# A two-layer hybrid backbone: layer 1's outputs with two 64-token parts in one stationary tile, gates in runs of 32 tokens by expert pairs, another order in the first mixer's heads

## The chip, the cores and the metric

The kernel runs on one core of one Trainium2 chip. The metric is the device time of one execution in microseconds (us); lower is better.

## What is computed

Two layers over 256 latent tokens with 256 context tokens beside them, width 1024, float32. Layer 0 mixes tokens by a bidirectional gated linear recurrence (HGRN2, 8 heads of 128), layer 1 by sliding-window attention. Behind each mixer stands a PEER channel mixer: 8 heads pick 16 of 16384 experts for each token by product keys, and every chosen expert has one row of `u` and one of `v`. The core of the reference:

```python
def chunk(h):
    t = h.shape[0]
    q = (h @ wq).reshape(t, PEER_HEADS, 2, PEER_DQ // 2)
    s = jnp.einsum('thpd,hpnd->thpn', q, sub_keys).astype(F32)
    sv, si = lax.top_k(s, PEER_TOPK)
    ...
    idx = jnp.take_along_axis(cand_i, best, axis=-1)
    gate = jax.nn.softmax(best_s, axis=-1)
    act = jax.nn.gelu(jnp.einsum('td,thkd->thk', h, u[idx]).astype(F32))
    return jnp.einsum('thk,thkd->td', (gate * act).astype(v.dtype), v[idx])
```

Each sub-layer is `x <- LayerNorm(ALPHA * x + gate * f(x * (1 + scale) + shift))`, where the modulation comes from a product of the condition with `mod_w`.

## The kernel before

Everything is written out for each engine, with semaphores between them. Products with float32 accuracy are made of two parts: a tile is split into a high part (a copy in the reduced format fp32r, ScalarE) and a low part (the difference, VectorE or GpSimd), and three products high x high, high x low, low x high are summed.

**The heads of the first mixer** (`head` in each engine's program). For head h TensorE does the recurrence by 8 levels (line 896 and 890) and, between them, projects the next head: `proj_piece` (line 842, 12 products of 512 columns for each half of four column blocks) and `value_piece` (line 855, 24 products in four parts of six). Level l of VectorE multiplies queries and keys by their decays (lines 1683 to 1685), merges the level's products (1686), and ScalarE copies the keys for the next level (1279). Behind the levels follow key transposes (904), their copies (1295), state products (915), the states on VectorE (1703, 1705), the head's outputs (929), squares (1298) and their sums (935); `scale_head` and `finish` (1713) close a head. VectorE also makes eight sums of a modulation row with the condition (`mod_sum`, 1616) in each head, and `low_w` (1600), the low part of the next weights. SyncE loads a modulation row's block (565) as soon as the sum that frees its slot is made, and the weights of the head after next (573).

**PEER in full.** The chosen experts are spread over nearly all of the 16384, so for most tokens the kernel multiplies with every expert and weighs with a gate that is zero where an expert isn't chosen. 128 blocks of 128 experts pass by. The tokens for which this is done are 384 in layer 0 and 192 in layer 1 (`ND`); the others (128 and 64) gather their chosen rows by indirect loads (`rows`, 2263 and 2273), which VectorE multiplies and adds (2012, 2019, 2029, 2035) in the same loop. A step of the loop for block j: `u` and `v` are loaded (639, 641; SyncE's queue waits for `u_lo` before the next u and for `v_lo` before the next v, in this order); scores of block j+1 on TensorE (1032), GELU on ScalarE (1478), times the gates on VectorE (1995) into `prod`, its high part on ScalarE (1483) and low part on VectorE (1999); `u_hi`, `v_hi` on ScalarE (1391, 1481), `u_lo`, `v_lo` on VectorE (1975, 1997); then outputs of block j on TensorE, in layer 0 with the tokens as stationary operand (1092, moving 512 columns of v), in layer 1 with v as stationary operand (1086, moving 192 tokens), so that layer 1's result `yT` lies turned. The scores of the first `KA` = 24 blocks are made earlier, so that each layer's first 24 steps have outputs only.

**Gates.** A loop over 16 tokens at a time builds one-hot rows (VectorE 1970, 1971; weighed on ScalarE 1442 and GpSimd 2255), TensorE multiplies them (1075), ScalarE stores the products to `gb` (1455), and SyncE spills `gb` to the DRAM tensor `gd` (666). Within a block of experts `gb` and `gin` hold, for each of 32 tokens (`GCH`), four expert columns side by side. The last 32 tokens' gates are copied on chip (1489).

**The end.** Layer 1's `yT` is copied from its banks (ScalarE 1516, VectorE 2134), turned back (1124) and the 64 + 64 folded tokens joined (1120, 1127), then two blocks are normalised (1768 and following) and stored.

## Time and profile before

| | |
|---|---|
| runs shown | 2957.34, 2962.82, 2963.38 us; median 2962.82 us |
| profiled execution | 2962.92 us, its span 2961.1 us |
| TensorE busy | 2739.6 us (93%), mean granted clock 0.964 |
| VectorE busy | 2330.2 us (79%) |
| ScalarE busy | 1148.5 us (39%) |
| GpSimd busy | 847.1 us (29%) |
| HBM read, written | 635.31 MB, 45.92 MB; 230 GB/s over the span |
| chain that ended last | TensorE 17%, DMA 3%, VectorE 3% of the span |

Busy time is what the engine's instructions took; matmuls overlap, so that a full TensorE need not be at its peak. The chain of waits follows each step back to what released it, and covers the last part of the execution only. Engines are named PE (TensorE matmul), PEld (its weight load), DVE (VectorE), ACT (ScalarE), POOL (GpSimd) and SP (SyncE); SPq is its queue of transfers.

### The profile page before, as it was taken

What the parts mean: (1) busy time and instruction counts of PE and PEld (TensorE: products, weight loads), DVE (VectorE), ACT (ScalarE), POOL (GpSimd) and SP (SyncE); (2) the same over time, 40 slices, a digit from 0 to 9 for tenths busy, and PEclk for the clock granted to TensorE, in tenths of its full rate; (3) what the DMA queues carried; (4) which work ended last, traced back from release to release, by engine and by line L of the source; (5) the groups of instructions that cost most, each with busy time, mean ns of one, the idle gap of its engine ahead of it and who ended that gap; (6) DMA issues with size and microseconds to landing.
All of it is one profiled execution on the core that took longest, in us unless ns stands there. A gap on an engine that the chain in (4) does not pass through costs nothing. (4 is left out here: it accounts for less than half of the span.)

```text
span 2961.1 us, 46261 instructions
## 1 busy us (share of the span) xinstructions
PE 2739.6 (93%) x16594; PEld 2421.1 (82%) x16594; DVE 2330.2 (79%) x4148; ACT 1148.5 (39%) x1889; POOL 847.1 (29%) x565
## 2 busy tenths in 40 slices
PE   7999978899788999999999999798987899999997
PEld 3778864689777899999999999554887899999997
DVE  2788876799998778788888888743898877787887
ACT  2233320433583333333333333233446344444443
POOL 0000001435453344443333333000664212222221
PEclk9999988999999999999999999899898999999999
DMA  6223224415479998888888888311266978888885
GB/s 252 106 83 117 78 100 155 158 51 168 140 220 376 330 333 308 307 303 311 317 303 307 303 315 308 122 58 69 103 191 202 388 278 311 310 312 314 308 314 193
DMA packets 247822, 682.42 MB, mean 230 GB/s; under 512 B 20172, under 2 KB 106804, under 8 KB 244020
## 3 DMA queue, kind: packets, MB, share of 16 engines
q1 hardware_dynamic: 192436, 479.96, 46.2%
q0 software_dynamic: 55296, 201.35, 19.0%
q8 instruction: 45, 0.74, 0.1%
q14 instruction: 45, 0.37, 0.0%
HBM read 635.31 MB, written 45.92 MB: 230 GB/s over the span
## 5 line engine op out<-in xcount | busy, mean ns | idle before, releaser
L1032 PE MATMUL bank<-h_parts,u_hi 128*128 128x384 f32 (+1 forms) x3712 | 799.2, 307 | 21.8 <-DVE u_lo L1975 12.2
L1032 PEld LDWEIGHTS bank<-h_parts,u_hi 128*128 128x128 f32 x3712 | 627.0, 192 | 32.5 <-issue 12.6
L1032 PE MATMUL bank<-h_parts,u_lo 128*128 128x384 f32 (+1 forms) x1856 | 569.8, 307 | 0.0
L1092 PE MATMUL bank<-v_parts,p_hi 128*128 128x512 f32 x1536 | 477.2, 392 | 7.4 <-DVE p_lo L1999 7.4
L1086 PE MATMUL bank<-p_hi,v_parts 128*128 128x192 f32 x2048 | 371.2, 278 | 9.1 <-DVE p_lo L1999 8.4
L1032 PEld LDWEIGHTS bank<-h_parts,u_lo 128*128 128x128 f32 x1856 | 356.5, 192 | 0.0
L1997 DVE TENSOR_TENSOR v_parts<-arena,v_parts 128x1024 fp32r<-128x1024 f32 x256 | 313.2, 1223 | 36.3 <-ACT v_parts L1481 31.5
L1092 PEld LDWEIGHTS bank<-v_parts,p_hi 128*128 128x128 f32 x1536 | 288.0, 189 | 64.0 <-issue 7.6
L1086 PEld LDWEIGHTS bank<-p_hi,v_parts 128*128 128x128 f32 x2048 | 325.9, 195 | 12.9 <-DVE p_lo L1999 7.2
L1975 DVE TENSOR_TENSOR u_lo<-arena,u_hi 128x1024 fp32r<-128x1024 f32 x208 | 254.7, 1225 | 93.6 <-ACT u_hi L1391 89.7
L1391 ACT ACTIVATE u_hi<-arena 128x1024 fp32r<-128x1024 f32 x208 | 219.7, 1056 | 269.7 <-DMA arena<-in_u 269.3
L1478 ACT ACTIVATE arena<-bank 128x384 f32<-128x384 f32 (+1 forms) x208 | 85.2, 410 | 560.0 <-PE bank L1032 559.5
L1092 PE MATMUL bank<-v_parts,p_lo 128*128 128x512 f32 x768 | 301.8, 393 | 0.0
L1481 ACT ACTIVATE v_parts<-arena 128x1024 fp32r<-128x1024 f32 x256 | 269.6, 1053 | 78.4 <-PE bank L1092 47.1
L1995 DVE TENSOR_TENSOR arena<-arena 128x384 f32<-128x384 f32 (+1 forms) x256 | 175.3, 685 | 158.3 <-ACT arena L1478 144.2
L2263 POOL DMA_INDIRECT arena<-in_v,arena x128 | 197.1, 1540 | 320.9 <-DVE arena L2019 297.0
L1086 PE MATMUL bank<-p_lo,v_parts 128*128 128x192 f32 x1024 | 283.3, 277 | 0.0
L2263 POOL DMA_INDIRECT arena<-in_ug,arena x128 | 181.9, 1421 | 260.6 <-DVE arena L2012 237.2
L1086 PEld LDWEIGHTS bank<-p_lo,v_parts 128*128 128x128 f32 x1024 | 199.4, 195 | 0.0
L1075 PE MATMUL bank<-arena 128*128 128x128 f32 x1152 | 149.5, 285 | 33.7 <-DVE arena L1971 19.2
L1075 PEld LDWEIGHTS bank<-arena 128*128 128x128 f32 x1152 | 138.3, 197 | 45.2 <-ACT arena L1442 45.2
L842 PE MATMUL bank<-h_parts,u_hi 128*128 128x512 f32 x512 | 165.9, 405 | 5.0 <-DVE u_lo L1600 5.0
(308 smaller groups left out, 4630.4 us busy)
## 6 DMA issues: line engine op xcount, KB each, us to landing
arena<-in_u SPq DMA_DIRECT2D x256, 512.0 KB, 5.2
arena<-in_v SPq DMA_DIRECT2D x256, 512.0 KB, 4.4
arena<-in_wm SPq DMA_DIRECT2D x80, 512.0 KB, 4.2
arena<-in_wst SPq DMA_DIRECT2D x19, 2048.0 KB, 7.9
gate_scratch<-arena SPq DMA_DIRECT2D x18, 2048.0 KB, 8.7
arena<-gate_scratch SPq DMA_DIRECT2D x30, 768.0 KB, 6.6
arena<-in_whd SPq DMA_DIRECT2D x8, 2560.0 KB, 9.2
arena<-gate_scratch SPq DMA_DIRECT2D x30, 384.0 KB, 5.2
```

What stands on the lines that cost most here:

```text
L842: last = mm(out, w[:, k, :], x, start=(k == 0 and i == 0), stop=(k == KT - 1 and i == 2))
L1032: last = mm(banks[q][:, 0:ND[p]], w[:, q, col], h[:, k, DS[p]], start=(n3 == 0), stop=(n3 == 3 * KT - 1))
L1075: last = mm(out, tiles8(oh_i, q)[:, t, :], tiles8(oh_j, q)[:, t, :], start=True, stop=True)
L1086: last = mm(out, x[:, q, c * P:(c + 1) * P], y[:, q, 0:n_t], start=(first and i == 0 and c % 2 == 0), stop=(final and i == 2), skip_group_ ...
L1092: last = mm(banks[2 + 2 * b + half][:, :], x[:, q, b * P:(b + 1) * P], y[:, q, col], start=(first and i == 0), stop=(final and i == 2))
L1391: af_(u_hi[:, q, :], u_raw[:, q, :], ACT.Copy).then_inc(u_h[q], 1)
L1478: af_(act_s[:, q, 0:ND[p]], banks[q][:, 0:ND[p]], ACT.Gelu_apprx_tanh).then_inc(s_act[q], 1)
L1481: af_(v_hi[:, q, :], raw[:, q, :], ACT.Copy).then_inc(v_h[q], 1)
L1975: V.tensor_tensor(u_lo[:, q, :], u_raw[:, q, :], u_hi[:, q, :], ALU.subtract).then_inc(u_l[q], 1)
L1995: V.tensor_tensor(prod[:, q, 0:ND[p]], (act_s[:, q] if own else act_ring[r % 4])[:, 0:ND[p]], gates[:, 0:ND[p], r % 4], ALU.mult).then_inc ...
L1997: V.tensor_tensor(v_lo[:, q, :], raw[:, q, :], v_hi[:, q, :], ALU.subtract).then_inc(v_l[q], 1)
L2263: G.indirect_dma_start(rows[:, c, :], None, a["ug"].rearrange("l e d -> (l e) d") if x < PH * TOPK else a["v"].rearrange("l j i d -> (l j ...
```

## The change

Three things change.

1. Layer 1's outputs take the tokens as stationary operand. The high part of the 192 weights and the low part stand in one tile `p_parts`; its columns 192 to 319 (`p_two`) hold a second copy of the first 64 tokens' high part and, directly behind it, their low part. A product of `p_two` with `v_hi` and one with `v_lo` gives both parts' contributions on separate output rows of banks 4 and 5; the other 128 tokens have the three products on banks 2 and 3. At the end `foldw` adds the two row halves.
2. Gates lie as `(expert pair, token, 2)` in runs of 32 tokens.
3. In the heads of the first mixer some products and sums stand elsewhere.

```diff
         h_hi, h_lo = h_parts[:, 0, :, :], h_parts[:, 1, :, :]
-        p_hi = sb("p_hi", [P, 2, ND_MAX], F32R)
-        p_lo = sb("p_lo", [P, 2, ND_MAX], F32R)
+        p_parts = sb("p_parts", [P, 2, 2 * ND_MAX], F32R)
...
-        gb = ar(B_HF, 8192, s=2, j=NK // 4, t=GCH, f=4)
+        gb = ar(B_HF, 8192, s=2, n=NK // 2, t=GCH, f=2)
...
+        PL = [ND_MAX, 256]
...
+        def p_hi(p):
+            return p_parts[:, :, 0:ND[p]]
+        def p_lo(p):
+            return p_parts[:, :, PL[p]:PL[p] + ND[p]]
+        p_two = p_parts[:, :, ND[1]:ND[1] + P]
...
                     if l == 0:
                         pe.wait_ge(init, h + 1)
-                    if more:
+                    if more and l != 1:
                         proj_piece(h + 1, l // 2, l % 2)
...
                     last.then_inc(lvl, 1)
+                    if more and l == 1:
+                        proj_piece(h + 1, 0, 1)
+                if more:
+                    value_piece(h + 1, 0, 2)
                 pe.wait_ge(upd, 7 * h + 7)
...
                     last.then_inc(kt_pe, 1)
                 if more:
-                    value_piece(h + 1, 0)
+                    value_piece(h + 1, 2, 3)
...
                     last.then_inc(ds, 1)
-                    if more:
-                        value_piece(h + 1, 1 + d)
+                if more:
+                    value_piece(h + 1, 3, 6)
...
                 if more:
-                    value_piece(h + 1, 3)
+                    value_piece(h + 1, 6, KT)
...
                     if p:
-                        n_t = ND[p]
-                        for c in range(KT):
-                            out = banks[2 + c // 2][:, (c % 2) * n_t:(c % 2 + 1) * n_t]
-                            for i, (x, y) in enumerate(((v_hi, p_hi), (v_hi, p_lo), (v_lo, p_hi))):
-                                last = mm(out, x[:, q, c * P:(c + 1) * P], y[:, q, 0:n_t], start=(first and i == 0 and c % 2 == 0),
-                                          stop=(final and i == 2), skip_group_check=True)
-                    for b in range(0 if p else nd):
+                        for half in range(2):
+                            for i, y in enumerate((v_hi, v_lo)):
+                                mm(banks[4 + half][:, :], p_two[:, q, :], y[:, q, 512 * half:512 * half + 512],
+                                   start=(first and i == 0), stop=(final and i == 1))
+                    for b in range(nd - p):
                         for half in range(2):
                             col = slice(half * 512, half * 512 + 512)
-                            for i, (x, y) in enumerate(((p_hi, v_hi), (p_hi, v_lo), (p_lo, v_hi))):
-                                last = mm(banks[2 + 2 * b + half][:, :], x[:, q, b * P:(b + 1) * P], y[:, q, col],
+                            at = p * HALF + b * P
+                            for i, (x, y) in enumerate(((p_hi(p), v_hi), (p_hi(p), v_lo), (p_lo(p), v_hi))):
+                                last = mm(banks[2 + 2 * b + half][:, :], x[:, q, at:at + P], y[:, q, col],
                                           start=(first and i == 0), stop=(final and i == 2))
...
-                    pe.wait_ge(modT_a, 5)
-                    pe.wait_ge(at_oc, 11)
-                    for c in range(KT):
-                        last = nc.tensor.transpose(banks[c // 4][:, (c % 4) * P:(c % 4 + 1) * P], yT[:, c, P:2 * P], ident)
-                    last.then_inc(y_pe, 1)
...
+                    for half in range(2):
+                        last = mm(banks[6 + half][:, :], foldw[:, 0:P], y_two[:, 512 * half:512 * half + 512], start=False, stop=True)
...
-                        dst = gb[:, c, :, t0:t0 + 4, :].rearrange("p j t f -> p t j f")
+                        dst = gb[:, c, :, t0:t0 + 4, :].rearrange("p n t f -> p t n f")
...
+                    if p:
+                        af_(p_two[:, q, 0:HALF], prod[:, q, 0:HALF], ACT.Copy)
...
             def levels(h, slot, more, more2):
+                mod_sum(h, 0, 0)
                 if more:
                     low_w(h + 1, 1 - slot, 1)
-                mod_sum(h, 0, 0)
...
-                    if l % 2:
+                    if l in (1, 3, 5):
                         mod_sum(h, 2 + l // 4, (l // 2) % 2)
...
                 finish(h, slot)
+                mod_sum(h, BLOCKS_M - 1, 1)
...
-                    V.memset(yT[:, :, 0:HALF], 0.0).then_inc(at_oc, 1)
...
-                    norms(3, LN_BASE[p], LAST, lambda i, half: banks[6 * i + half][:, :], lambda b: 1, [8 + Y_BLOCK[1][1] + 1, 8 + Y_BLOCK[1][1] + 2])([0, 1])
+                    norms(3, LN_BASE[p], LAST, lambda i, half: banks[2 + 4 * i + half][:, :], lambda b: 1, [0, 8 + Y_BLOCK[1][1] + 1])([0, 1])
```

The multiply by the gates is rewritten to `gates[:, 0:ND[p] // GCH, (r % 4) // 2, :, r % 2]`: before, a step's gate of one token lay four numbers from the next token's, now two.

TensorE, in a head of the first mixer, from behind the key transposes (line 904, then 915) to the sums of squares (935, then 946). The value products of the next head are at line 855, then 863; the state products at 915, then 926; the outputs at 929, then 940. Before:

```order
L855 MATMUL bank<-h_parts,v_parts 128x512 x6
L911 REGISTER_ALU
L912 REGISTER_ALU
L915 MATMUL bank<-arena 128x128 x3
L855 MATMUL bank<-h_parts,v_parts 128x512 x6
L915 MATMUL bank<-arena 128x128 x3
L855 MATMUL bank<-h_parts,v_parts 128x512 x6
L929 MATMUL bank<-arena 128x128 x10
L855 MATMUL bank<-h_parts,v_parts 128x512 x6
L935 MATMUL bank<-const,arena 128x1 x4
```

and now, from the value products in front of the transposes:

```order
L863 MATMUL bank<-h_parts,v_parts 128x512 x6
L915 MATMUL bank<-const,arena 128x128 x3
L912 REGISTER_ALU
L915 MATMUL bank<-const,arena 128x128 x3
L863 MATMUL bank<-h_parts,v_parts 128x512 x3
L922 REGISTER_ALU
L923 REGISTER_ALU
L926 MATMUL bank<-arena 128x128 x6
L863 MATMUL bank<-h_parts,v_parts 128x512 x9
L940 MATMUL bank<-arena 128x128 x10
L863 MATMUL bank<-h_parts,v_parts 128x512 x6
L946 MATMUL bank<-const,arena 128x1 x4
```

Six value products now stand ahead of the transposes, three between them and the state products, and nine between the state products and the outputs.

TensorE at the end of layer 1's loop: the last output products of layer 1 (line 1086, then 1095 and 1102) and the joining of the folded tokens. Before:

```order
L1086 MATMUL bank<-p_lo,v_parts 128x192
L1086 MATMUL bank<-p_hi,v_parts 128x192 x2
L1086 MATMUL bank<-p_lo,v_parts 128x192
L1086 MATMUL bank<-p_hi,v_parts 128x192
L1120 MATMUL bank<-arena 128x512 x2
L1124 MATMUL bank<-const,arena 128x128 x8
L1127 MATMUL bank<-const,arena 128x128 x8
```

and now, for the last two blocks of experts:

```order
L1095 MATMUL bank<-v_parts,p_parts 128x512 x4
L1102 MATMUL bank<-v_parts,p_parts 128x512 x6
L1095 MATMUL bank<-v_parts,p_parts 128x512 x4
L1102 MATMUL bank<-v_parts,p_parts 128x512 x6
L1130 MATMUL bank<-arena 128x512 x2
L1134 MATMUL bank<-arena 128x512 x2
```

A block has ten products of 512 columns instead of 24 of 192, and the sixteen products that turned the result back are replaced by two.

VectorE from a head's end (`finish` 1713, then 1721) into the next head's start; a conditioning sum is line 1616, then 1624. Before:

```order
L1713 SCALAR_TENSOR_TENSOR arena<-bank,small,arena 128x512
L1722 REGISTER_ALU
L1724 ISA
L1724 TENSOR_TENSOR modcol<-small,modcol 128x8
L81 REGISTER_ALU
L1599 REGISTER_ALU
L1600 TENSOR_TENSOR u_lo<-arena,u_hi 128x1024
L1612 ISA
L1613 REGISTER_ALU
L1616 ISA v_parts,small<-arena 128x1024
L1616 ISA small 128x1
```

and now, from the same place:

```order
L1721 SCALAR_TENSOR_TENSOR arena<-bank,small,arena 128x512
L1624 ISA v_parts,small<-arena 128x1024
L1624 ISA small 128x1
L1731 REGISTER_ALU
L1733 ISA
L1733 TENSOR_TENSOR modcol<-small,modcol 128x8
L81 REGISTER_ALU
L1620 ISA
L1621 REGISTER_ALU
L1624 ISA v_parts,small<-arena 128x1024
L1624 ISA small 128x1
```

One sum stands behind the head's end now, and the next head's first sum stands ahead of `low_w`.

## Rows read from the trace of the kernel before

**Rows 1.** Windows, layer 0's and layer 1's expert loop: busy us of each engine, clock, DMA, GB/s

```profile
1030.00:1400.00 370.00, 370.00 (x1875) 337.17 (x1874) 296.10 (x395) 131.45 (x180) 160.82 (x109) 1.00 0.89 314
2850.00:2900.00 50.00, 50.00 (x450) 50.00 (x450) 40.52 (x48) 24.82 (x39) 12.72 (x10) 1.00 0.90 310
```

**Rows 2.** Chain that ended last, layer 1's loop: start, length (us), work

```profile
2393.98 2.68 PE bank L1032 x24
...
2849.84 2.68 PE bank L1086 x24
...
2932.92 2.69 PE bank L1032 x24
```

**Rows 3.** Timeline, VectorE and TensorE, one head: start, length, engine, line, operation [idle before]

```profile
318.22 0.75 DVE L1713 SCALAR_TENSOR_TENSOR arena<-bank,small,arena 128x512 f32 x1
...
332.24 1.23 PE L896 MATMUL bank<-arena 128*128 128x128 f32 x8 [1.12 <-ACT arena L1279]
...
353.50 0.88 PE L904 MATMUL bank<-const,arena 128*128 128x128 f32 x6 [1.55 <-DVE arena L1685]
...
358.25 1.64 PE L855 MATMUL bank<-h_parts,v_parts 128*128 128x512 f32 x6
359.72 2.42 PE L929 MATMUL bank<-arena 128*128 128x128 f32 x20
...
363.35 0.75 DVE L1713 SCALAR_TENSOR_TENSOR arena<-bank,small,arena 128x512 f32 x1
```

**Rows 4.** Timeline, TensorE in layer 0's loop: first output and first score products

```profile
1507.21 0.63 PE L1092 MATMUL bank<-v_parts,p_hi 128*128 128x512 f32 x2
1511.33 0.51 PE L1032 MATMUL bank<-h_parts,u_hi 128*128 128x384 f32 x2
```

**Rows 5.** Timeline, one step of layer 1's loop, by engine

```profile
2853.42 0.34 SPq L639 DMA_DIRECT2D arena<-in_u  x1
2858.06 1.06 ACT L1391 ACTIVATE u_hi<-arena 128x1024 fp32r<-128x1024 f32 x1 [1.29 <-DMA arena<-in_u]
2859.71 1.23 DVE L1975 TENSOR_TENSOR u_lo<-arena,u_hi 128x1024 fp32r<-128x1024 f32 x1
2863.08 0.38 PE L1032 MATMUL bank<-h_parts,u_hi 128*128 128x192 f32 x2
```

**Rows 6.** Transfers of 2400 to 2900 us, and the chain's longest landing there

```profile
DMA packets 43362, 154.95 MB, mean 310 GB/s; under 512 B 4814, under 2 KB 4814, under 8 KB 43355
arena<-in_u SPq DMA_DIRECT2D x93, 512.0 KB, 5.3
...
2427.64 7.59 DMA arena<-in_u
```

**Rows 7.** Windows and transfers at the start of layer 1's experts

```profile
2308.00:2330.00 22.00, 21.66 (x178) 20.46 (x179) 22.00 (x39) 10.90 (x15) 6.78 (x7) 1.00 1.03 401
...
arena<-in_v SPq DMA_DIRECT2D x23, 512.0 KB, 9.1
```

**Rows 8.** Groups by line and shape: busy us, mean ns | idle before

```profile
L1997 DVE TENSOR_TENSOR v_parts<-arena,v_parts 128x1024 fp32r<-128x1024 f32 x256 | 313.2, 1223 | 36.3 <-ACT v_parts L1481 31.5
...
L1455 ACT ACTIVATE arena<-bank 128x512 f32<-128x512 f32 x144 | 76.8, 579 | 4.0 <-PE bank L1075 3.9
...
L1995 DVE TENSOR_TENSOR arena<-arena 128x192 f32<-128x192 f32 x128 | 64.9, 507 | 24.7 <-ACT arena L1478 17.6 <-DMA arena<-gate_scratch 6.1
...
L1999 DVE TENSOR_TENSOR p_lo<-arena,p_hi 128x192 fp32r<-128x192 f32 x128 | 45.1, 352 | 0.0
```

**Rows 9.** Timeline, VectorE at a head's first level

```profile
328.70 0.69 DVE L1683 TENSOR_TENSOR arena<-arena 128x512 f32<-128x512 f32 x1 [0.44 <-PE bank L896]
329.31 1.15 DVE L1684 TENSOR_TENSOR arena<-arena 128x512 f32<-128x512 f32 x1
```

**Rows 10.** Timeline, VectorE at the kernel's end

```profile
2941.47 1.02 DVE L2134 COPY arena<-bank 128x384 f32<-128x384 f32 x2 [0.43 <-PE bank L1086]
2944.15 1.29 DVE L1768 TENSOR_TENSOR arena<-bank,arena 128x512 f32<-128x512 f32 x2 [1.66 <-PE bank L1124]
```

More of the change, by code:

```diff
@@ L65 @@
 C_KEEP, C_ALL = 384, 1024 + 256
-C_SHIFT, C_FOLD, C_END = C_ALL, C_ALL + 192, C_ALL + 192 + 128
+C_SHIFT, C_FOLD, C_END = C_ALL, C_ALL + 192, C_ALL + 192 + 192
 HALF = P // 2
@@ L334, in build @@
         oh_j = ar(6144, 2048, s=2, d=D)
-        gin = ar(4096, 3072, s=2, t=ND_MAX, f=4)
-        gin_first = [ar(at, 4 * ND_MAX, t=ND_MAX, f=4) for at in (B_Q, B_M)]
+        gin = ar(4096, 3072, s=2, c=ND_MAX // GCH, h=2, t=GCH, f=2)
+        gin_first = [ar(at, 4 * ND_MAX, c=ND_MAX // GCH, h=2, t=GCH, f=2) for at in (B_Q, B_M)]
         act_s = ar(8192, 768, s=2, t=ND_MAX)
@@ L348, in build @@
         s20 = ar(9984, 20)
-        yT = ar(A_HD, 2 * D, c=KT, t=2 * P)
+        y_two = ar(A_HD, D)
         shift = ar(B_T + 1152, 192)
-        foldw = ar(B_T + 1536, P)
-        assert B_T + 1536 + P <= AW and A_HD + 2 * D <= A_LN
+        foldw = ar(B_T + 1536, P + HALF)
+        assert B_T + 1536 + P + HALF <= AW and A_HD + D <= A_LN
         p16 = ar(10004, 16)
@@ L665, in spill @@
                     rows = gate_rows(c)[:, j0:j1, :]
-                    sp.dma_start(rows, gb[:, c % 2, j0:j1, :, :].rearrange("p j t f -> p j (t f)")).then_inc(g_out[c % 2], 16)
+                    sp.dma_start(rows, gb[:, c % 2, 2 * j0:2 * j1].rearrange("p (j h) t f -> p j (h t f)", h=2)).then_inc(g_out[c % 2], 16)
                 for c in range(C):
@@ L844, in proj_piece, with value_piece @@
                     last.then_inc(proj, 1)
-            def value_piece(g, part):
+            def value_piece(g, k0, k1):
                 w_hi, w_lo = weight_parts(2)
-                if part == 0:
+                if k0 == 0:
                     pe.wait_ge(hw_l, 5 * g + 5)
@@ L852, in value_piece @@
                         pe.wait_ge(vsb, 2 * g)
-                for k in range(2 * part, 2 * part + 2):
+                for k in range(k0, k1):
                     for i, (w, x) in enumerate(((w_hi, h_hi[:, k, :]), (w_hi, h_lo[:, k, :]), (w_lo, h_hi[:, k, :]))):
                         last = mm(banks[7][:, :], w[:, k, :], x, start=(k == 0 and i == 0), stop=(k == KT - 1 and i == 2))
-                if part == 3:
+                if k1 == KT:
                     last.then_inc(vproj, 1)
@@ L868, in _ @@
                     proj_piece(0, c, half)
-            for part in range(4):
-                value_piece(0, part)
+            value_piece(0, 0, KT)
             def head(h, slot, more):
@@ L1119, in peer @@
                     for half in range(2):
-                        mm(banks[6 + half][:, :], foldw, y_tok[:, 512 * half:512 * half + 512], start=True, stop=False, skip_group_check=True)
-                    pe.wait_ge(modT_a, 5)
-                    pe.wait_ge(at_oc, 11)
-                    for c in range(KT):
-                        last = nc.tensor.transpose(banks[c // 4][:, (c % 4) * P:(c % 4 + 1) * P], yT[:, c, P:2 * P], ident)
-                    last.then_inc(y_pe, 1)
-                    for c in range(KT):
-                        last = mm(banks[6 + c // 4][:, (c % 4) * P:(c % 4 + 1) * P], yT[:, c, 0:P], ident, start=False, stop=True, skip_group_check=True)
+                        mm(banks[6 + half][:, :], foldw[:, HALF:HALF + P], y_tok[:, 512 * half:512 * half + 512], start=True, stop=False)
+                    pe.wait_ge(modT_a, 4)
+                    pe.wait_ge(at_oc, 9)
+                    for half in range(2):
+                        last = mm(banks[6 + half][:, :], foldw[:, 0:P], y_two[:, 512 * half:512 * half + 512], start=False, stop=True)
                     last.then_inc(y_pe, 1)
@@ L1514, in peer @@
                     act.wait_ge(y_ac[1], 1 + PAIRS * 2)
-                    for x in range(2):
-                        af_(yT[:, 2 * x:2 * x + 2, HALF:2 * P], banks[2 + x][:, 0:2 * ND[p]].rearrange("p (c t) -> p c t", c=2), ACT.Copy).then_inc(modT_a, 1)
+                    af_(y_two[:, 0:512], banks[4][:, :], ACT.Copy).then_inc(modT_a, 1)
             peer(0)
@@ L1763, in front @@
                     st = stat[:, (i % 4) * 20:(i % 4) * 20 + 20]
-                    if y_need:
+                    if y_need and y_need[i]:
                         dve.wait_ge(y_pe, y_need[i])
@@ L1994, in step @@
                         dve.wait_ge(g_first, 2 * p + slot + 1)
-                    V.tensor_tensor(prod[:, q, 0:ND[p]], (act_s[:, q] if own else act_ring[r % 4])[:, 0:ND[p]], gates[:, 0:ND[p], r % 4], ALU.mult).then_inc(p_do[q], 1)
+                    weights, gelus = (x[:, 0:ND[p]].rearrange("p (c t) -> p c t", t=GCH) for x in (prod[:, q], act_s[:, q] if own else act_ring[r % 4]))
+                    V.tensor_tensor(weights, gelus, gates[:, 0:ND[p] // GCH, (r % 4) // 2, :, r % 2], ALU.mult).then_inc(p_do[q], 1)
                     dve.wait_ge(v_h[q], N + 1)
@@ L2132, in peer @@
                     dve.wait_ge(y_ac[1], 1 + PAIRS * 2)
-                    for x in range(2):
-                        V.tensor_copy(yT[:, 4 + 2 * x:6 + 2 * x, HALF:2 * P], banks[4 + x][:, 0:2 * ND[p]].rearrange("p (c t) -> p c t", c=2)).then_inc(at_oc, 1)
+                    V.tensor_copy(y_two[:, 512:1024], banks[5][:, :]).then_inc(at_oc, 1)
                 if p == 0:
```

14 lines of the change are left out of this document (7 added, 7 removed).

## The prediction, made before the changed kernel ran

> **What bounds the kernel now.** I read the views in this order: busy time by stretch, to see which engine is full in which stage; the chain that ended last, for the step of layer 1's expert loop; the timeline of one step there and of one head; the groups by shape for the prices; and the transfers of two stretches.
>
> Layer 0's expert loop is full on TensorE: 370.00 of 370 us, VectorE at 296 [rows 1]. Its matmuls do not change, so a faster multiply on VectorE buys nothing there. Layer 1's loop is full on TensorE too, 50.00 of 50 us, while VectorE is busy 40.5 and the transfers run at 310 GB/s [rows 1]. Its step is 24 score products and 24 output products of 192 columns, 2.68 us each set; from 2393.98 to 2932.92 there are 100 steps, so 5.389 us a step, against 2 x 2.68 = 5.36 if nothing ever waited [rows 2]. TensorE thus loses 3 us in 100 steps.
>
> The first mixer's heads repeat every 363.35 - 318.22 = 45.13 us, and in each TensorE stands still twice: 1.12 us before the second level's products, 1.55 us before the key transposes [rows 3]. The rest of a head is matmuls.
>
> **Part 1, layer 1's outputs.** Removed in each of 128 steps: 24 matmuls of 192 columns, 2.68 us [rows 2]. That is 112 ns each although they have few columns to stream. Added: ten of 512 columns, four with the 64 tokens' high and low halves side by side as one stationary tile, six for the other 128 tokens. Layer 0 has this shape: 18 of them take 1511.33 - 1507.21 = 4.12 us, or 229 ns each [rows 4]. Ten cost 2.29 us, so the step would be 2.68 + 2.29 = 4.97 us. The Trainium skill (TensorE: Matmul & The Clock Gate, "Wait — 56ns, not 53.3ns?") puts a matmul at N / 2.4 GHz + 2.5 ns, 216 ns for 512 columns; by it ten would cost 2.16 us, the step 4.84, and the loop 13 us less than by the row. No row here shows 216, so I keep the row's 229.
>
> Who is late next? VectorE's work of a step is 40.5 / 50 x 5.36 = 4.3 us [rows 1], so it isn't VectorE. It is the u block. In the step shown it is issued at 2853.42, ScalarE starts on it at 2858.06, VectorE ends u_lo at 2859.71 + 1.2 = 2860.9, and TensorE takes it at 2863.08, 2.2 us later [rows 5]. The issue follows v_lo of step j (SyncE waits for it at line 641 before the next u) and the use is the scores of step j + 3, so the allowance is three steps less a fixed part. Three steps of 0.39 us less take 1.17 us from it. Issue to use is 9.66 us here; less 1.06 for u_hi and 1.2 for u_lo, a landing of up to 7.4 us is borne now, and 6.2 to 6.5 then. The median landing is 5.3 us and single ones take 7.59 [rows 6]. Pairing each of the loop's issues with ScalarE's start on that block, as in [rows 5], I count 12 of 95 above 6.5 us, together 7.4 us over: 0.08 us a step. Landings also lengthen with traffic: a step moves 310 GB/s x 5.389 us = 1.67 MB [rows 6], so 326 GB/s at 5.13 us. At 401 GB/s, in layer 1's first steps, a block lands after 9.1 us [rows 7]; between (310, 5.3) and (401, 9.1) that is about 0.6 us more at 326, which brings the loss to some 0.16 us a step. I take 5.13 us: 5.389 - 5.13 = 0.26 us, x 100 = **26 us**. The ends: 42 us if no block is ever late (4.97), 0 if the landing holds the old pace.
>
> The other 24 steps, at layer 1's start, have outputs only. There VectorE is busy 22.00 of 22 us and the transfers run at 401 GB/s with a share over 1 [rows 7]. TensorE isn't the bound and the bytes stay: 0 us. Layer 1's ScalarE gets one more copy a step (64 columns); it costs less than the 579 ns of a 512-column copy and runs while VectorE makes v_lo (1223 ns), so 0 us [rows 8]. If that cover went, up to 0.58 us x 100 would be at stake.
>
> **Part 2, gates by pairs.** The multiply reads a gate each 16 bytes now and takes 507 ns for 192 columns, against 352 for the same-sized subtraction with dense reads [rows 8]. It will read each 8 bytes. A VectorE product of 512 columns with such reads takes 0.69 us [rows 9], no more than dense ones, so I expect about 0.35 us: 0.15 us off VectorE in layer 1, 0.3 in layer 0. VectorE sets neither loop, so 0 us. The gate stage's ScalarE stores write runs of two numbers instead of four; 579 ns now [rows 8]. I take no change, since runs of two appear in the levels without loss; the other end is below, among the rivals.
>
> **Part 3, heads.** (a) Six value products (358.25 to 359.72, 1.47 us [rows 3]) move in front of the key transposes, into the wait of 1.55: 1.47 us gained. They must not be missed later: behind the state products nine now stand in one run (2.2 us) where VectorE computes the states, so the outputs still find TensorE the last. (b) At level 1 the products of the next head go behind the level's own. VectorE's 0.44 us wait for these [rows 9] goes, the next key copy comes as much earlier, and TensorE's 1.12 us shrink to about 0.7: 0.44 us. (c) On VectorE one conditioning sum goes from before the states to behind the head's end, another fills a wait at the head's start. VectorE holds no end there: 0 us, but the sum frees the 1.2 us that (a) needs. Its weight row's load is issued that much later, on SyncE's queue just ahead of the next head's 2.5 MB; it is used some 6 us later, so hidden. Together 1.9 us x 7 heads = **13.3 us**. Ends: 0 and 2.67 x 7 = 18.7 us.
>
> **Part 4, the end.** Block 3's norm reads its banks directly instead of waiting 1.66 us for the turned-back block, and one bank copy of about 0.5 us is gone from VectorE (two took 1.02) [rows 10]: about **2.2 us**; ends 0 and 2.7. One clearing write goes from the loop, once; I leave it out.
>
> Sum: 26 + 13.3 + 2.2 = 41.5 us off the profiled execution's 2962.92 us (2961.1 its span), which equals the median of 2962.82 within 0.1: **2921 us**.
>
> **The rivals.**
> (B) The u blocks are never late. For: after each late one the spare recovers within two steps. Against: the 7.59. Loop 42 us, total 57.5: 2905 us.
> (C) The transfers hold the loop. For: in the step shown ScalarE stands 1.29 us until u has landed [rows 5], and the traffic rises as the step shortens. Against: 401 GB/s is reached elsewhere [rows 7], at which 1.67 MB need 4.2 us. If the landings lengthen so much that the step stays near 5.33, the loop gives 6 us and the total is 21.5: 2941 us. The Trainium skill (DMA: Bandwidth & Descriptors, "Where 436 GB/s comes from") puts the limit of loads from HBM near 358 GB/s a core, which would put (C) closer: 1.67 MB would need 4.7 us. The trace disagrees, with 401 GB/s over 22 us.
> (D) The heads' waits only move, as VectorE becomes their last: 2934 us.
> (E) Slower: the gate stores with runs of two. The steepest row for short runs is VectorE's first level, 1.15 us against 0.69, where every element lies apart [rows 9]. At that ratio a store takes 0.97 us, +0.39 x 144 = 56 us with nothing hidden, and the total is 2977 us. It decides from 42 / 144 = 0.29 us a store. Against: later levels, with runs of two and more, do not show it. The Trainium skill (SBUF — State Buffer, "Door 1: The DMA port swizzle (why `[64,N]` ≈ `[32,N]`)") speaks of 16-byte lines that need two hits for full bandwidth; by it runs of two numbers stay at full speed, and the 16-byte reads of the multiply, one hit each, are the slow ones, with which the 507 ns agree.
>
> **How the numbers follow.** Forecast 0.58, (B) 0.17, (C) 0.15, (D) 0.05, (E) 0.05. What a measurement of this kernel can tell from no change is about 0.2%, 6 us. All but (E) are faster by more; a part of (C) might fall within, were the heads to fail with it: faster 0.92, same 0.03, slower 0.05. The range reaches from a little below (B), 2903, to a little above (C), 2945.
>
> **What would show it.** Right: layer 1's outputs at 2.3 us for ten matmuls; the loop's step 5.0 to 5.25 us, with TensorE's waits there on VectorE's u_lo, and ScalarE waiting for in_u before them; the multiply near 0.35 us; a head of 43.2 us; layer 0's outputs unchanged at 4.12 us; stores near 579 ns; the end 2 us shorter. Wrong: a step of 5.33 with long waits for in_u (C), stores above 0.8 us (E), heads at 45 (D), or matmuls of 512 columns at another price than 229 ns behind those of 192.

## The result, and the profile after

| | before | changed |
|---|---|---|
| median of the runs | 2963.1 us (4 runs, 2957.3 to 2965.3) | 2944.1 us (4 runs, 2941.0 to 2947.5) |
| profiled execution, and its span | 2962.92, 2961.1 | 2943.2, 2941.4 |
| ratio of changed to before | | 0.9936, 95% interval 0.9920 to 0.9952 |

The change takes 19 us off, 14 to 24 by the interval. 41.5 were forecast. The profile's page of the changed kernel, its busy times and the chain that ended last:

```profile
PE 2698.3 (92%) x14782; PEld 2307.4 (78%) x14782; DVE 2279.4 (77%) x4146; ACT 1159.3 (39%) x2016; POOL 849.8 (29%) x565
...
DMA 9%; PE 6%; DVE 5%; issue 3%; ACT 2%; SPq 1%; DVEq 0%; ACTq 0%; POOLq 0%
DMA arena<-in_u 7%; PE bank L1043 3%; DVE v_parts L2007 2%; PE bank L1102 1%; ACT u_hi L1398 1%; PE bank L1095 1%; DVE u_lo L1984 1%; ACT v_parts L1488 1%; DVE arena L2039 1%; PE bank L1086 1%; DVE arena L1980 0%; DMA arena<-gate_scratch 0%; DVE arena L2005 0%; SPq L649 0%; DMA arena<-in_v 0%
```

Before, TensorE was 17% of the span in that chain. Now the load of u leads it with 7%. The windows say the same, in the columns of [rows 1]: layer 0's loop is as full as it was, layer 1's no longer.

```profile
1200.00:1570.00 370.00, 370.00 (x1871) 336.71 (x1870) 291.74 (x371) 127.72 (x180) 148.58 (x98) 1.00 0.88 308
2850.00:2900.00 50.00, 48.85 (x326) 43.26 (x326) 39.07 (x50) 27.59 (x50) 11.90 (x10) 1.00 0.89 320
```

Taken step by step from the starts of the score products, an undisturbed step of layer 1's loop is 4.96 us, as forecast. But the last 100 steps, up to the one that starts at 2915.47, take 524.9 us, 5.249 each, against 5.389 before: 14 us saved, not 26. 24 of these steps are over 5.26 us, and 15 of these stand at a multiple of four steps from each other: 28.9 us are lost in the hundred, where before it was 2.9.

The 19.7 us between the two profiled spans lie as follows: 0.6 are there when layer 1's outputs begin (2286.9 before, 2286.3 now), 2.7 come up to the last 100 steps, 14.0 in these, 2.4 behind the last scores. So in this pair of profiles next to nothing of the heads' gain had come through to layer 1's outputs, though the heads themselves did what was forecast. VectorE and TensorE, one head, the timeline's columns as in [rows 3]:

```profile
309.03 0.74 DVE L1721 SCALAR_TENSOR_TENSOR arena<-bank,small,arena 128x512 f32 x1
...
322.66 1.23 PE L903 MATMUL bank<-arena 128*128 128x128 f32 x8 [0.64 <-ACT arena L1286]
...
343.93 0.87 PE L915 MATMUL bank<-const,arena 128*128 128x128 f32 x6 [0.16 <-DVE arena L1693]
...
352.22 0.74 DVE L1721 SCALAR_TENSOR_TENSOR arena<-bank,small,arena 128x512 f32 x1
```

A head takes 352.22 - 309.03 = 43.19 us. The waits of 1.12 and 1.55 us [rows 3] have become 0.64 and 0.16, and the last head ends at 440.7 instead of 454.6: 13.9 us. The groups by shape for the multiply, the gate stores and the added copy [rows 8], and VectorE at the end [rows 10]:

```profile
L2005 DVE TENSOR_TENSOR arena<-arena 128x192 f32<-128x192 f32 x128 | 45.2, 353 | 10.5 <-DMA arena<-gate_scratch 7.7 <-ACT arena L1485 2.8
...
L1462 ACT ACTIVATE arena<-bank 128x512 f32<-128x512 f32 x144 | 78.6, 594 | 4.0 <-PE bank L1086 3.8
...
L1491 ACT ACTIVATE p_parts<-arena 128x64 fp32r<-128x64 f32 x128 | 32.8, 256 | 41.6 <-DVE arena L2005 40.2
```

```profile
2923.83 0.69 DVE L2142 COPY arena<-bank 128x512 f32<-128x512 f32 x1
2924.44 1.28 DVE L1777 TENSOR_TENSOR arena<-bank,arena 128x512 f32<-128x512 f32 x2
```

The multiply went from 507 to 353 ns, the stores from 579 to 594, and at the end one bank copy and the wait of 1.66 us are gone.

Two questions: what holds the u blocks back, and where do 14 us of the heads go?

### The profile page after: what moved, and what is told of

It is laid out like the page before. It is cut to its first block and busy times, and to the rows that moved or that the text cites. A ratio compares the mean times of both kernels' runs of the same rounds, so it can differ in the third digit from the quotient of the medians.

```text
span 2941.4 us, 42761 instructions
## 1 busy us (share of the span) xinstructions
PE 2698.3 (92%) x14782; PEld 2307.4 (78%) x14782; DVE 2279.4 (77%) x4146; ACT 1159.3 (39%) x2016; POOL 849.8 (29%) x565
## 5 line engine op out<-in xcount | busy, mean ns | idle before, releaser
L1102 PE MATMUL bank<-v_parts,p_parts 128*128 128x512 f32 x3072 | 747.0, 393 | 8.9 <-DVE p_parts L2009 8.9
L1102 PEld LDWEIGHTS bank<-v_parts,p_parts 128*128 128x128 f32 x3072 | 580.0, 189 | 129.3 <-issue 7.3
L2271 POOL DMA_INDIRECT arena<-in_v,arena x128 | 198.9, 1554 | 319.0 <-DVE arena L2029 295.2
L2271 POOL DMA_INDIRECT arena<-in_ug,arena x128 | 176.1, 1376 | 270.7 <-DVE arena L2022 246.6
L2005 DVE TENSOR_TENSOR arena<-arena 128x384 f32<-128x384 f32 (+1 forms) x256 | 117.0, 457 | 150.9 <-ACT arena L1485 132.5
L1086 PE MATMUL bank<-arena 128*128 128x128 f32 x1152 | 150.0, 286 | 33.2 <-DVE arena L1980 19.7
L2029 DVE SCALAR_TENSOR_TENSOR arena<-arena 128x1024 f32<-128x1024 f32 x128 | 164.0, 1281 | 6.8
L1095 PE MATMUL bank<-v_parts,p_parts 128*128 128x512 f32 x512 | 147.0, 410 | 16.5 <-DVE p_parts L2009 16.5
L2022 DVE CUSTOM_DVE_ANT_0 arena<-arena 128x1024 f32<-128x1024 f32 x128 | 151.4, 1219 | 2.8 <-DMA arena<-in_ug,arena 2.8
L2281 POOL DMA_INDIRECT arena<-in_v,arena x64 | 74.2, 1160 | 264.6 <-DVE arena L2045 240.2
L2281 POOL DMA_INDIRECT arena<-in_ug,arena x64 | 81.7, 1276 | 211.3 <-DVE arena L2039 207.4
```

What stands on the lines that cost most here:

```text
L1086: last = mm(out, tiles8(oh_i, q)[:, t, :], tiles8(oh_j, q)[:, t, :], start=True, stop=True)
L1095: mm(banks[4 + half][:, :], p_two[:, q, :], y[:, q, 512 * half:512 * half + 512], start=(first and i == 0), stop=(final and i == 1))
L1102: last = mm(banks[2 + 2 * b + half][:, :], x[:, q, at:at + P], y[:, q, col], start=(first and i == 0), stop=(final and i == 2))
L2029: V.scalar_tensor_tensor(y_tok, rows[:, x % RING_G, :], p16[:, x:x + 1], y_tok, ALU.mult, ALU.add).then_inc(row_use[x % RING_G], 1)
L2271: G.indirect_dma_start(rows[:, c, :], None, a["ug"].rearrange("l e d -> (l e) d") if x < PH * TOPK else a["v"].rearrange("l j i d -> (l j ...
L2281: G.indirect_dma_start(rows[:, c, :], None, a["ug"].rearrange("l e d -> (l e) d") if x < HALF else a["v"].rearrange("l j i d -> (l j i) d" ...
```

## The experiments: which part gives what

All ratios are against the kernel before, run beside them on the same chip.

**e1, the heads alone.** The kernel before, with only this part of the change:

```diff
 def head(h, slot, more):
-    if more:
+    if more and l != 1:
         proj_piece(h + 1, l // 2, l % 2)
...
+    if more and l == 1:
+        proj_piece(h + 1, 0, 1)
+ if more:
+    value_piece(h + 1, 0, 2)
  pe.wait_ge(upd, 7 * h + 7)
...
-    if l % 2:
+    if l in (1, 3, 5):
         mod_sum(h, 2 + l // 4, (l // 2) % 2)
...
  finish(h, slot)
+ mod_sum(h, BLOCKS_M - 1, 1)
```

> The kernel before with the heads' part of the change alone (order of the next head's products and of the conditioning sums); outputs and gates as before. Both theories expect a head of 43.2 us and wout's start about 14 us earlier, as in the changed kernel. Theory S (swallowed): the later stages (key scores and top-k with GpSimd, the outputs-only steps at the transfers' pace) wait for something that the heads do not move, so little of it reaches the end: -1 to -4 us, and the last scores of layer 0's loop start no more than 3 us earlier than before. Theory F (forecast): the 13.3 us arrive at the end, -11 to -15 us, and what the changed kernel lost behind the heads was lost by its own gate stage and outputs.

Measured: 2949.8 us median of 5, ratio 0.9948 (0.9935 to 0.9961), so 12 to 19 us faster. Theory S falls: in its profile the last output product of layer 0's loop starts 7.0 us earlier than in the kernel before (1857.1 against 1864.1), where theory S allowed 3. The heads' gain does reach the end, at least its greater part.

**e2, all but the heads.** The changed kernel with the diff of e1 taken back.

> The changed kernel with the heads as before. Theory S: almost the changed kernel's time, -15 to -19 us against the kernel before. Theory F: the heads carry about 13 us of the change's 19, so only about -6 us are left.

Measured: 2954.7 us median of 10 (2944.7 to 2963.6), ratio 0.9971 (0.9957 to 0.9985), so 4 to 13 us faster. Outputs, gates and end together give some 9 us, where 28.2 were forecast. In its profile layer 1's step is 5.303 us. Its runs spread over 19 us, which would fit a loop that hangs on single landings; no run shows that this is the reason.

**e3, the gates alone.** The kernel before with the layout of `gin` and `gb` changed, and the multiply:

```diff
-gb = ar(B_HF, 8192, s=2, j=NK // 4, t=GCH, f=4)
+gb = ar(B_HF, 8192, s=2, n=NK // 2, t=GCH, f=2)
...
-... gates[:, 0:ND[p], r % 4], ALU.mult)
+... gates[:, 0:ND[p] // GCH, (r % 4) // 2, :, r % 2], ALU.mult)
```

> The kernel before with the gates in runs by expert pairs alone. The multiply falls from 507 to 353 ns (192 columns) and from 863 to 561 (384). Forecast: no effect on the time, within 3 us, since VectorE sets neither loop. Rival: the stores in runs of two (594 against 579 ns) lie on the gate stages' path, 144 x 15 ns = 2 us slower, to +5 us; and if the multiply lies on the way from the transfers to the products, 3 to 8 us faster.

Measured: ratio 1.0003 (0.9994 to 1.0011). The multiply takes 355 and 560 ns, a store 592, and the time stands still. VectorE's saved time is worth nothing in either loop.

**e9, the changed kernel again**, to see how far it scatters.

> The changed kernel itself, word for word, beside the others: how far its own time scatters. Expected 2941 to 2948 us, within the interval seen. With the same kernel without the heads' part at 2954.7 it says what the heads are worth at the end: 10 us or more bears out the forecast's term of 13.3, under 5 us would not.

Measured: 2940.1 us median of 6 (2932.5 to 2954.0), ratio 0.9916 (0.9897 to 0.9934), 1 us below the expected 2941 to 2948. Against e2 that is 14.6 us less, and it agrees with the sum of e1 and e2. The profiled execution was its slowest, 2954.0. Its profile once more shows nothing of the heads' gain where layer 1's outputs begin (2291.6 us). But these two profiles are the exception: with the heads' change the outputs begin at 2275.1 to 2281.4 us in the eight others, and without it at 2285.5 to 2287.7 in all four. So one pair of profiles can mislead by several us about what a part is worth. Here the many runs decide, and they give the heads 12 to 19 us and the rest 4 to 13.

## The experiments: what makes the u blocks late

The trace of the changed kernel shows a stall. SyncE's queue, and then ScalarE, VectorE and TensorE with the block whose load is issued last here:

```profile
2653.78 0.33 SPq L649 DMA_DIRECT2D arena<-in_v  x1
2654.31 0.33 SPq L643 DMA_DIRECT2D arena<-gate_scratch  x1
2654.84 0.33 SPq L647 DMA_DIRECT2D arena<-in_u  x1
```

```profile
2663.38 1.06 ACT L1398 ACTIVATE u_hi<-arena 128x1024 fp32r<-128x1024 f32 x1 [4.10 <-DMA arena<-in_u]
```

```profile
2664.47 1.23 DVE L1984 TENSOR_TENSOR u_lo<-arena,u_hi 128x1024 fp32r<-128x1024 f32 x1 [3.14 <-ACT u_hi L1398]
```

```profile
2665.75 0.47 PE L1043 MATMUL bank<-h_parts,u_hi 128*128 128x192 f32 x2 [1.98 <-DVE u_lo L1984]
```

Two things stand in front of this u: the wait for v_lo with v's 512 KB behind it, and 384 KB of gates, which are loaded every fourth step. ScalarE can start on it only 8.5 us after its issue. I paired all issues of the loop with ScalarE's starts. The 23 blocks right behind a gates load take 6.64 us in the mean, the 67 others 5.59. In the kernel before it was 6.43 (23) and 5.27 (69). I had read this spread as scatter; it has a period. Where TensorE's lateness falls says the same: the steps that use the 23 blocks behind gates carry 17.8 of some 28 us lost.

**e4, u issued ahead of the wait for v_lo.** Bytes and buffers stay; only SyncE's order in layer 1's loop changes (one load ahead of the loop, none of u in its last step):

```diff
+def experts_ahead(j, q, N):
+    nq, nN = 1 - q, N + q
+    sp.wait_ge(u_l[nq], 1 + nN)
+    sp.dma_start(u_raw[:, nq, :], a["u"][p, j + 1]).then_inc(u_in[nq], 16)
+    sp.wait_ge(v_l[q], 1 + N)
+    sp.dma_start(v_raw[:, q, :], a["v"][p, j]).then_inc(v_in[q], 16)
```

> The changed kernel, with each u block of layer 1's loop issued on SyncE before the wait for v_lo that it stood behind, some 2 us earlier; same bytes, same buffers. Theory L (landing: the block has too little time from issue to use): the step falls from 5.25 to 4.97-5.08 us, 17 to 28 us over 100 steps, and the time is 2917 to 2927 us. Theory B (bytes: 16 DMA engines cannot move 1.67 MB a step faster beside the gathers): the step stays at 5.2 to 5.3, the time within 3 us of 2944, and ScalarE waits for in_u or in_v as long as now.

Measured: 2909.1 us median of 5, ratio 0.9807 (0.9795 to 0.9820), 35 us below the changed kernel's first median and 31 below that of e9. That is more than theory L forecast (2917 to 2927). The step is 4.967 us over the last 100, one of them late. SyncE's queue and ScalarE in its profile:

```profile
2645.15 0.33 SPq L654 DMA_DIRECT2D arena<-in_u  x1
2647.35 0.33 SPq L656 DMA_DIRECT2D arena<-in_v  x1
```

```profile
2652.19 1.06 ACT L1413 ACTIVATE u_hi<-arena 128x1024 fp32r<-128x1024 f32 x1 [0.77 <-DMA arena<-in_u]
```

u now goes out 2.2 us ahead of v instead of 0.5 us or more behind it. ScalarE still waits for in_u, and the way from issue to its start isn't shorter, 6.8 us in the mean against 5.9: the wait has just moved to where it is covered. Theory L holds and B falls, since more bytes a second pass: 337 GB/s against 316. The windows from 2500 to 2850 us, of the kernel before, the changed one, e5 (below) and e4:

```profile
2500.00:2850.00 350.00, 349.47 (x3119) 348.61 (x3119) 283.55 (x357) 171.81 (x263) 82.39 (x65) 1.00 0.87 311
```

```profile
2500.00:2850.00 350.00, 336.05 (x2252) 301.06 (x2251) 274.45 (x362) 183.09 (x331) 75.22 (x66) 1.00 0.89 316
```

```profile
2500.00:2850.00 350.00, 344.00 (x2314) 308.07 (x2313) 281.68 (x370) 188.84 (x342) 76.70 (x68) 1.00 0.90 325
```

```profile
2500.00:2850.00 350.00, 349.59 (x2392) 320.74 (x2391) 296.53 (x379) 192.11 (x353) 110.19 (x71) 1.00 0.93 337
```

**e5, the gates behind the u block.** The changed kernel, with the wait and load of the gates called inside `experts`, between u and v:

```diff
 sp.dma_start(u_raw[:, q, :], a["u"][p, j]).then_inc(u_in[q], 16)
+if gate:
+    gate()
 sp.wait_ge(v_l[q], 1 + N)
```

> The changed kernel, but in layer 1's loop every fourth step's load of gates (384 KB) is issued behind that step's u block instead of ahead of it; the u block still stands behind the wait for v_lo. In the changed kernel the 23 u blocks issued just behind a gates load take 6.64 us from issue to ScalarE's start in the mean, the 67 others 5.59. Theory G (the queue: it is the 384 KB in front that make a u block late): these 23 fall to about 5.6, most stalls of every fourth step go, the step is 5.05 to 5.12 us, the time 2924 to 2934 us. Theory W (the wait for v_lo alone: a u block's time is too short wherever the gates stand): the stalls only move to other steps, within 4 us of 2944.

Measured: 2924.9 us median of 5, ratio 0.9882 (0.9867 to 0.9897), 19 us below the changed kernel's first median and 15 below that of e9. The step is 5.147 us, and 18.7 us are lost in 100 instead of 28.9. The time lies where theory G put it, the step above its 5.05 to 5.12. The same 23 blocks take 6.0 us instead of 6.6, not the 5.6 of the forecast, and the others 5.7 instead of 5.6. The loss in the steps that use these 23 falls from 17.8 to 5.4 us, and in the others it rises from 10.0 to 12.2. So each theory has a share: most of what the gates caused goes, and a part moves to other steps. The gates in front account for about a third of the loss by the profiles, for about half of e4's gain by the medians (0.3 to 0.4 of it by the ratios). The rest is the place behind the wait for v_lo.

**e6, the kernel before with the edit of e4.**

> The kernel before with u issued ahead of the wait for v_lo in layer 1's loop (the edit of e4 without the change). The step stands at TensorE's 5.36 us already, with 3 us lost in 100 steps. If e4's 35 us are slack that only the shorter step needs, this gives -1 to -4 us against the kernel before. If e4's gain were something else (less traffic at a time, fewer collisions), it would show here too, with more than -8 us.

Measured: ratio 0.9991 (0.9982 to 1.0000), median 2960.6 of 12. The step is 5.364 us, TensorE's pace. The same edit that is worth 31 to 35 us behind the change is worth 3 without it (0 to 5 by the interval): the old step hid the late blocks.

**e8, both.** e4, and the gates between u and v.

> e4 with the gates load issued behind the u block as well. Its step is at TensorE's 4.96 us in all but one place, so nothing is left to take: within 3 us of e4's 2909. If v blocks had become late behind the earlier u, it would be slower by some us.

Measured: 2906.3 us median of 5, ratio 0.9817 (0.9803 to 0.9832). The same as e4 within what can be told. e4 and e8 beat both kernels by far: 54 to 58 us below the kernel before, by the medians.

**e7, two output products fewer**, to see how far the transfers could follow. It leaves out one of the three terms for the last 128 tokens.

```diff
-for i, (x, y) in enumerate(((p_hi(p), v_hi), (p_hi(p), v_lo), (p_lo(p), v_hi))):
+products = ((p_hi(p), v_hi), (p_hi(p), v_lo), (p_lo(p), v_hi))[:3 - p]
+for i, (x, y) in enumerate(products):
```

> e4 with two of layer 1's ten output products of a step left out: the product of the low weights with the high v rows for the last 128 tokens (they are missing from the output). TensorE's step is then 2.68 + 8 x 0.229 = 4.51 us, VectorE's work in it stays near 4.2. Theory B (bytes hold just below e4's pace): 1.67 MB in 4.51 us would be 370 GB/s; if the transfers stop at some 340 to 360 GB/s, the step is 4.65 to 4.9 and TensorE waits for u or v. Theory R (room left): the step is 4.51 to 4.6, -36 to -45 us in the loop against e4, and the transfers run at 360 to 370 GB/s. The Trainium skill (DMA: Bandwidth & Descriptors, 'Where 436 GB/s comes from') has the loads of a core at about 358 GB/s, by which theory B would hold, at 4.66 us.

Measured: 2883.5 us median of 4, ratio 0.9741 (0.9726 to 0.9755). The step is 4.654 us over the last 100, 4.51 undisturbed.

```profile
2500.00:2800.00 300.00, 295.40 (x2058) 266.86 (x2057) 266.33 (x348) 179.49 (x325) 89.06 (x65) 1.00 0.96 359
```

Between the two theories, and nearer to B: most steps run at 4.51, but some in each stretch are late, and the mean stays at 359 GB/s, with a share of 0.96. So 6% below e4's step something beside TensorE begins to hold. The Trainium skill (DMA: Bandwidth & Descriptors, "Where 436 GB/s comes from") has about 358 GB/s for the loads of a core. The mean here comes out at that number, but it is no ceiling for this core, since 401 passed over 22 us [rows 7]. That the bytes are what holds is not shown. VectorE, busy 266 of 300 us, isn't far from full here either, and the time from a u block's issue to its use has fallen to 9.6 us in the mean, from 11.6 in e4. This run doesn't part the three.

## The experiments: the heads

**e10, level 1 as before.** The changed kernel with `if more and l == 1` taken back, so that the next head's products stand ahead of the level's own again.

> The changed kernel, but at level 1 the next head's products stand ahead of the level's own again, as before. Forecast: the wait ahead of the second level's products returns to about 1.1 us (0.64 in the changed kernel), and a head takes 43.6 us instead of 43.19. Rival: the wait is not set by that order, and the head stays at 43.2.

Measured in a single execution: the wait is 1.11 us again.

```profile
323.92 1.23 PE L903 MATMUL bank<-arena 128*128 128x128 f32 x8 [1.11 <-ACT arena L1284]
```

Of the seven distances between its head ends five are 43.61 to 43.96 us, where in the changed kernel five are 43.19 to 43.25. So the term of 0.44 us holds, in kind and in size. From the first head end to the last it is 307.5 us against 305.5, but that sum decides nothing: over the eight other profiles with the same heads it runs from 304.5 to 307.9, since now and then a head is about 1 us longer. (Its 2940.2 us of a single execution say nothing about 3 us.)

**e11, the last conditioning sum as before.**

```diff
-    if l in (1, 3, 5):
+    if l % 2:
         mod_sum(h, 2 + l // 4, (l // 2) % 2)
...
- mod_sum(h, BLOCKS_M - 1, 1)
```

> The changed kernel, but with VectorE's last conditioning sum of a head ahead of the states again instead of behind the head's end. Forecast (the sum frees the 1.2 us which the six value products in front of the key transposes need behind them): the state products' readers are late, and a head takes 44.0 to 44.4 us. Rival (VectorE had the time anyway): 43.2 to 43.4.

Measured in a single execution (2939.3 us): five of the seven distances are 43.50 to 43.54 us, 0.3 longer than in the changed kernel and between the forecast and the rival. VectorE at the first state behind TensorE's state products, in the changed kernel and then in e11:

```profile
303.02 0.29 DVE L1711 COPY arena<-bank 128x128 f32<-128x128 f32 x1 [0.59 <-PE bank L926]
```

```profile
303.25 0.28 DVE L1711 COPY arena<-bank 128x128 f32<-128x128 f32 x1
```

In the changed kernel VectorE still waits 0.59 us for the products there; in e11 it comes last itself. So the sum's new place is worth about 0.3 us a head, less than the 0.8 to 1.2 expected, and the value products' gain hangs on it only in this part.

**Where profiles lose what the heads gain.** At the first early scores the profiles with the heads' change are still 9 to 15 us ahead. In the stretch from there to the gates' one-hot rows VectorE selects experts while GpSimd computes low parts. It takes 115.8 us in the kernel before and 120.8 in e1 and in the changed kernel (119.5 in e2, so that it isn't the heads' change alone that can lengthen it). The windows of before and of e1 over it:

```profile
655.60:771.40 115.80, 105.39 (x585) 104.01 (x585) 110.90 (x382) 36.90 (x52) 60.29 (x23) 0.94 0.47 157
```

```profile
641.50:762.30 120.80, 107.83 (x585) 106.45 (x585) 115.91 (x382) 36.83 (x52) 60.14 (x23) 0.92 0.46 150
```

VectorE executes the same 382 instructions and is busy 5.01 us longer, which is the whole difference. Single ones stretch. GpSimd and VectorE of e1, and then the same two operations in the kernel before:

```profile
710.56 2.40 POOL L2252 TENSOR_TENSOR u_lo<-arena,u_hi 128x1024 fp32r<-128x1024 f32 x1 [3.15 <-ACT u_hi L1403]
```

```profile
711.01 2.51 DVE L1919 CAST arena<-arena 128x1024 f32<-128x1024 uint32 x1
```

```profile
719.67 2.40 POOL L2248 TENSOR_TENSOR u_lo<-arena,u_hi 128x1024 fp32r<-128x1024 f32 x1 [0.29 <-ACT u_hi L1400]
```

```profile
723.26 0.68 DVE L1915 CAST arena<-arena 128x1024 f32<-128x1024 uint32 x1
```

The copy that takes 0.68 us alone takes 2.51 when a GpSimd operation began 0.45 us ahead of it, and ends 0.56 us after that one's end (712.96). In seven of the nine profiles with the heads' change before e12 the copy is hit so (2.51 to 2.56 us), in e8's and e11's it takes 0.68, as in all four without. The stretch goes with it: from the first early scores to the one-hot rows it is 120.7 or 120.8 us in all seven, and 115.6 and 115.8 in e11 and e8, though these have the heads' change too. The window of e8:

```profile
645.40:761.30 115.90, 105.48 (x585) 104.10 (x585) 111.00 (x382) 36.88 (x52) 60.31 (x23) 0.94 0.48 157
```

Of the 5 us the copy itself has 1.9; in the same profiles other operations of VectorE stretch too, one of 4096 columns from 5.16 to 6.48 us. (The expectation below counts ten and three, one too many.) The Trainium skill (SBUF — State Buffer, "SBUF: two separate sides") says that VectorE and GpSimd share a pair of ports, and that the one which starts first, on VectorE's side an operation in a two-port mode or with two inputs in SBUF, holds it for the whole instruction while the other blocks. The trace agrees.

**e12, the copy moved.** e8, with this copy ahead of the sum, the reciprocal and the product that it followed:

```diff
+link(V.tensor_copy(si..., siu...))
 dve.wait_ge(ex_a, p + 1)
 link(V.tensor_reduce(gsf, bsf, AX.X, ALU.add))
```

> e8 with one of VectorE's copies (uint32 to float, 1024 columns, in layer 0's selection of experts) moved 1.2 to 2 us earlier, ahead of the sum, reciprocal and product it followed. In the profiles of seven of the ten kernels with the heads' change this copy takes 2.5 us and ends 0.55 us after the GpSimd operation that began up to 0.5 us before it; in the three others and in all without that change it takes 0.68, and the stretch from the first early scores to the gates is 5 us shorter. Theory K (VectorE stands still while GpSimd's operation holds what they share; which copies are hit is a matter of phase): the copy takes 0.68 us there and the stretch is 115.5 to 117 us; the time is 0 to 5 us below e8's 2906. Rival (the copy is a symptom, the stretch is longer for another reason, such as the granted clock): the copy is short and the stretch is still 120 to 121 us.

Measured: 2909.5 us median of 5, ratio 0.9820 (0.9805 to 0.9835), e8's time. The stretch takes 117.6 us, but the copy isn't short. GpSimd and VectorE:

```profile
704.73 2.40 POOL L2283 TENSOR_TENSOR u_lo<-arena,u_hi 128x1024 fp32r<-128x1024 f32 x1 [0.30 <-ACT u_hi L1431]
708.88 2.89 POOL L2283 TENSOR_TENSOR v_parts<-arena,v_parts 128x1024 fp32r<-128x1024 f32 x1 [1.76 <-ACT v_parts L1434]
```

```profile
705.50 2.17 DVE L1939 CAST arena<-arena 128x1024 f32<-128x1024 uint32 x1
...
709.55 2.31 DVE L1948 COPY arena<-arena 128x128 f32<-128x128 f32 x1
```

Both signs of theory K failed, the copy of 0.68 us and the stretch of at most 117, and the rival's too. The copy met another GpSimd operation, and ended 0.54 us after it (707.13). A copy of 128 columns was hit as well, and GpSimd's operation beside it took 2.89 us instead of 2.40. That fits the rule, read afterwards, and it shows that moving one operation doesn't free the stretch. Which ones are hit seems a matter of phase; a remedy would have to take work off one of the two engines there, and wasn't tried. The changed kernel's profile loses in two more places. Between the last head and the first early scores it loses 3.7 us, nearly all in the stretch that starts with the key scores, where TensorE is busy 103.6 of 109.2 us before and 105.7 of 112.7 now. In the four profiles with a mean granted clock of 0.95 or 0.96 there (the changed kernel, e8, e9, e11) this stretch takes 112.0 to 112.9 us, in the ten others, at 0.98, 109.2 to 110.3. In layer 0's experts it loses 4.3; that differs from one profile to the next of equal code, and its cause stays open.

## Why the prediction was wrong where it was

**The step that failed** is the size of a term in part 1, "I take 5.13 us: 5.389 - 5.13 = 0.26 us, x 100 = 26 us". The mechanism was named rightly: TensorE's pace is 4.96 (4.97 forecast), the u block is late next, its issue stands behind the wait for v_lo, and ScalarE waits for in_u. The size was wrong: in the profiles the term of 26 us came out as 14.0, and as 8.6 in e2's (5.389 - 5.303 = 0.086 us, x 100). A loss of 0.16 us a step was reckoned, and it is 0.29 in the profile (5.249 - 4.96), 0.34 in e2's. Three parts of that estimate erred, all to the same side.
- The allowance was given as 6.2 to 6.5 us, and the count of late blocks was made at the upper end. It differs from block to block. The four blocks of the changed kernel's trace with three undisturbed steps before their use have 7.96 to 8.86 us from issue to use; less 1.06 and 1.23 for the two parts that is 5.7 to 6.6. In the changed kernel's 90 pairs the excess over 6.25 us is 21.8 us, over 5.95 it is 31.6: the measured 0.29 a step lies between.
- The late blocks were taken for scatter. A third to a half of the matter is the gates load in front of every fourth one, which could be read from the kernel before (6.43 against 5.27 us).
- Twelve blocks over 6.5 us, together 7.4 us over, were counted in the kernel before; a full pairing finds 15 of 92 and 10.5 us.

From issue to ScalarE's start the blocks did take longer, by 0.2 to 0.3 us instead of the 0.6 reckoned, but those reckoned 0.6 had been turned into only 0.08 us a step.

**(B), u never late, 2905 us,** is what e4 and e8 make of the kernel by one more edit: 2906 to 2909. **(C), the transfers hold the loop, 2941 us,** names nearly the time that came, for the wrong reason: the step was 5.25, not 5.33, and e4 moves the same bytes at 337 GB/s. **(D)** falls: the heads' waits went and stayed away. **(E)** falls: a store takes 594 ns, not 970, and e3 gives 1.0003.

**What was right.** Layer 1's ten products at 229 ns, and the first 24 steps without a loss. The gates: the multiply at 353 ns (about 350 forecast), nothing in the time. The heads: 43.2 us forecast, 43.19 measured, and 13.3 us forecast against 12 to 19 by e1. In (a) 1.39 us of the 1.47 were won, in (b) 0.48 of 0.44. For (c) nothing was reckoned, and the sum's place was to free the 1.2 us that (a) needs; by e11 it is worth 0.3 us a head. The end: 2.2 forecast, 2.4 measured. The extra copy of 256 ns a step cost nothing that can be seen, though no run took it out.

By terms: heads 13.3 against about 15, outputs and end 28.2 against about 9. The range of 2903 to 2945 held the 2944.1, by little. The changed kernel's second series (2940.1) lies somewhat lower, still far from 2921.

## What to carry to other kernels

When a step gets shorter, every prefetch loses that much time for each step it reaches ahead (here from 9.66 us between issue and use [rows 5] to 7.96 to 8.86 in undisturbed steps). Compute the new allowance at its short end, and look at what stands in front of each load on its queue, by period as well as by mean. A queue that waits for the later of two buffers before it refills the earlier one costs nothing while the step is long; swapping the two was worth 31 to 35 us here once the step was short, and 3 before. And a gain measured in place (13.9 us of heads) is to be priced by many runs with and without it, since a single pair of profiles had it vanish.

## What the runs showed of the hardware

A copy of VectorE's stretches from 0.68 to 2.5 us when a GpSimd operation on SBUF began just ahead of it, and ends 0.54 to 0.56 us after that one. Which operations are hit differs from profile to profile, and a stretch of 116 us takes 5 us more or less with it; in seven profiles it took 120.7 or 120.8 us with the copy hit, in six 115.5 to 119.5 without. With a mean granted clock of 0.95 or 0.96 instead of 0.98 the stretch of the key scores took 112.0 to 112.9 us instead of 109.2 to 110.3. The transfers ran at 337 GB/s over 350 us with TensorE at its full pace, and at 359 GB/s over 300 us in e7, where some steps began to wait.
